# A hybrid decoder layer on one core: step lists per engine for the cross attention, and another order in the mixer's lists

## What is computed

```python
hn = rms_norm(h, norm1_g); proj = hn @ w_in
mix = concat([hgrn2_group(...4 heads...), swa_group(...8 heads, window 128...)]) @ w_out
h = h + mix
hn, mn = rms_norm(h, norm2_g), rms_norm(mem, mem_norm_g)
q = head_rms(hn @ wq, q_norm_g)                        # 4 heads of 128
k, v = head_rms(...mn @ wkv...), ...                   # 256 memory rows
p = softmax(q @ k.T * 128**-0.5)
h = h + (p @ v) @ wo
hn = rms_norm(h, norm3_g); a = relu(hn @ mlp_up)
h = h + (a * a) @ mlp_down
```

## Time and profile before

| | |
|---|---|
| median of 3 runs | 2525.46 us (2523.58 to 2527.55) |
| the profiled execution | 2525.87 us, of which the span of the profile is 2524.1 us |
| granted TensorE clock, mean over the span | 0.996 of 2.4 GHz |
| PE busy | 2465.3 us, 98% of the span |
| PE weight loads busy | 2016.1 us, 80% |
| DVE busy | 1742.6 us, 69% |
| ACT busy | 1138.6 us, 45% |
| POOL busy | 894.0 us, 35% |
| DMA | 371.54 MB, mean 147 GB/s |

### The profile page before, as it was taken

One profiled execution on the slowest core, in us unless ns is written; L12 is line 12 of the kernel. 1 busy time (PEld: TensorE's weight loads), 2 busy tenths in 40 slices (PEclk: granted clock), 3 DMA queues, 4 the chain that ended last, 5 costly groups with the idle time before them and its releaser, 6 DMA issues.

```text
span 2524.1 us, 39349 instructions
## 1 busy us (share of the span) xinstructions
PE 2465.3 (98%) x14110; PEld 2016.1 (80%) x14110; DVE 1742.6 (69%) x3014; ACT 1138.6 (45%) x2164; POOL 894.0 (35%) x1018
## 2 busy tenths in 40 slices
PE   7999999999998999899999999999999999999999
PEld 5877888888887778687878888788888888888887
DVE  6898788788678465666586866976664544566665
ACT  5565576576566356446563222532223233322331
POOL 1433100000001552465246767476673222222222
PEclk9999999999999999999999999999999999999999
DMA  4432633533642431642153344233347653444664
GB/s 185 167 119 103 213 132 120 209 127 120 211 133 105 175 117 59 241 176 76 53 202 109 122 155 158 88 118 127 116 138 268 216 162 107 140 128 148 212 192 142
DMA packets 186547, 371.54 MB, mean 147 GB/s; under 512 B 13937, under 2 KB 79985, under 8 KB 183665
## 3 DMA queue, kind: packets, MB, share of 16 engines
q1 hardware_dynamic: 181200, 359.51, 42.4%
q10 hardware_dynamic: 5152, 9.51, 1.0%
HBM read 286.71 MB, written 79.89 MB: 145 GB/s over the span
## 4 chain that ended last, share of the span: by engine, by line
PE 49%; POOL 5%; issue 5%; DVE 4%; ACT 2%; DMA 2%; SPq 0%; ACTq 0%; DVEq 0%; POOLq 0%
PE bank L3239 8%; PE bank L3241 8%; PE bank L3243 8%; PE bank L3219 4%; PE bank L3215 4%; PE bank L3216 4%; PE bank L2158 3%; PE bank L2153 3%; PE bank L2154 3%; POOL m_xlo L2706 2%; POOL wlo L2706 2%; DMA raw<-w_cross 1%; PE bank L2205 1%; PE bank L2184 1%; PE bank L2195 1%
## 5 line engine op out<-in xcount | busy, mean ns | idle before, releaser
L443 POOL TENSOR_TENSOR wlo<-raw,whi 128x256 fp32r<-128x256 f32 x372 | 326.4, 910 | 960.6 <-ACT whi L1145 520.7
L1538 PE MATMUL bank<-hi,whi 128*128 128x512 f32 x704 | 286.0, 406 | 2.1 <-ACT fg L1108 2.1
L3239 PE MATMUL bank<-hi,whi 128*128 128x512 f32 x896 | 275.8, 389 | 0.0
L3241 PE MATMUL bank<-lo,whi 128*128 128x512 f32 x896 | 275.8, 389 | 0.0
L3243 PE MATMUL bank<-hi,wlo 128*128 128x512 f32 x896 | 275.8, 389 | 0.0
L1541 PE MATMUL bank<-lo,whi 128*128 128x512 f32 x704 | 275.1, 391 | 0.0
L3030 DVE TENSOR_TENSOR lo<-h,hi 128x1024 fp32r<-128x1024 f32 x80 | 124.1, 1552 | 172.7 <-ACT hi L2794 172.6
L2725 POOL TENSOR_TENSOR wlo<-h,whi 128x256 fp32r<-128x256 f32 x160 | 128.8, 829 | 299.3 <-ACT whi L2786 299.3
L2153 PE MATMUL bank<-hi,whi 128*128 128x512 f32 x504 | 208.4, 414 | 13.0 <-DVE h L2046 6.4
L2154 PE MATMUL bank<-lo,whi 128*128 128x512 f32 x504 | 197.8, 393 | 0.0
L3241 PEld LDWEIGHTS bank<-lo,whi 128*128 128x128 f32 x896 | 168.2, 188 | 34.9
(11 more groups left out here) (401 smaller groups left out, 5582.3 us busy)
## 6 DMA issues: line engine op xcount, KB each, us to landing
h<-hidden_scratch SPq DMA_DIRECT2D x96, 512.0 KB, 4.2
raw<-w_mix SPq DMA_DIRECT2D x88, 512.0 KB, 4.2
raw<-w_cross SPq DMA_DIRECT2D x64, 512.0 KB, 3.5
raw<-w_mlp SPq DMA_DIRECT2D x64, 512.0 KB, 4.8
wlo<-mixer_lows_scratch SPq DMA_DIRECT2D x60, 512.0 KB, 3.6
hidden_scratch<-hT SPq DMA_DIRECT2D x116, 256.0 KB, 2.1
h<-w_mlp SPq DMA_DIRECT2D x112, 256.0 KB, 2.9
mixer_lows_scratch<-wlo SPq DMA_DIRECT2D x22, 512.0 KB, 3.0
```

What stands on the lines that cost most here:

```text
L443: last = pool.tensor_tensor(wlo[:, i, cols], raw[:, i, cols], whi[:, i, cols].bitcast(F32), ALU.subtract)
L1538: pe.matmul(out, w, hi[:, k, :], start=k == 0, stop=False)
L3239: pe.matmul(down_bank(i)[:], wh[:, cols], xh[:, i % 2, :], start=K == 0, stop=False)
L3241: pe.matmul(down_bank(i)[:], wh[:, cols], xl[:, i % 2, :], start=False, stop=False)
```

## The change

Mixer: 12 of the 15 lists of PE, ACT and DVE (those of all four blocks; the three start lists and POOL's stay) hold the same steps in another order. Cross: `cross_steps`, `last_squares_end` and `CROSS_WORK` go; `CROSS_ORDERS` has a list for each engine and turn, in which each of PE, ACT and DVE has only its own steps, and `cross_order` yields them. A "-" behind a step in the list of turn 1 means that it belongs to turn 0. No step, no instruction of a step, no wait, buffer or semaphore is added or removed; a wait's threshold stands in the step, so it moves with it. The lists of SP and POOL are the same, instruction by instruction. Lines behind the lists move by 4 (L2046 of before is L2050).

```diff
 ORDERS = {
     "PE": (
...
-        "m0.0 m0.1 s0.0 s0.1 n0 T0 m0.2 m1.0 m1.1 D0 s0.2 s0.3 m1.2 m2.0 m2.1 o0.0 o0.1 o0.2 o0.3 m2.2 L0 m3.0 n1 "
...
+        "m0.0 m0.1 T0 n0 s0.0 s0.1 D0 s0.2 s0.3 m0.2 m1.0 m1.1 m1.2 m2.0 m2.1 m2.2 o0.0 o0.1 o0.2 o0.3 V L0 m3.0 m3.1 "
...
-def cross_steps():
...
-CROSS_STEPS = [s for steps in cross_steps() for s in steps]
-CROSS_WORK = [(turn, s) if s[0] != "late" else (turn - 1, s[1:]) for turn in range(SEQ // TB // 2)
-              for s in CROSS_STEPS if turn or s[0] != "late"]
-CROSS_WORK = last_squares_end(CROSS_WORK)
...
+CROSS_ORDERS = {
+    "PE": (
...
+        "c1.0.0 c1.0.1 u0.2.1 m23.2 u0.3.0 p0.2.0 p0.2.1 n1.2 u0.3.1 c1.1.0 p0.3.0 p0.3.1 n1.3 m24.0 m24.1 m24.2 "
+        "m25.0 m25.1 m25.2 m26.0 m26.1 m26.2 u1.0.0 m27.0 m27.1 m27.2 u1.0.1 c1.1.1 c1.2.0 p1.0.0 p1.0.1 c1.2.1 "
...
+def cross_order(engine):
+
+    for turn, row in enumerate(CROSS_ORDERS[engine]):
+        for token in row.split():
+            step = token.rstrip("-")
+            yield turn - (step != token), (CROSS_NAMES[step[0]],) + tuple(int(n) for n in step[1:].split(".") if n)
...
-            for turn, step in CROSS_WORK:
+            for turn, step in cross_order("ACT"):
...
-            for turn, step in CROSS_WORK:
+            for turn, step in cross_order("DVE"):
...
-            for turn, step in CROSS_WORK:
+            for turn, step in cross_order("PE"):
```

More of the change, by code:

```diff
@@ L230 @@
 CROSS_PRODUCT_AT = {p[1:]: n for n, p in enumerate(CROSS_PRODUCTS)}
-def cross_steps():
-    def panels(role, b, first, end):
-        return list(panel_steps([CROSS_PANEL_AT[role, b, n] for n in range(first, end)],
-                                lambda i: [n for n, p in enumerate(CROSS_PRODUCTS) if p[0] == i]))
-    def squares(b):
-        return [[("norm_square", b, k)] for k in range(KT)]
-    def apply(b):
-        return [[("norm_apply", b, k)] + [("norm_low", b, k - 1)] * (k > 0) for k in range(KT)] + [[("norm_low", b, KT - 1)]]
-    def write(b):
-        return [[("norm_write", b, k)] + [("norm_store", b, k - 1)] * (k > 0) for k in range(KT)] + [[("norm_store", b, KT - 1)]]
-    def attend(b):
-        subs = [(b, u, q) for u in range(HEADS) for q in range(QT // 2)]
-        for n in range(len(subs) + 3):
-            if n < len(subs):
-                yield [("scores", *subs[n])]
-            if 0 <= n - 1 < len(subs):
-                yield [("scale", *subs[n - 1])] + [("turn", *subs[n - 2])] * (n > 1)
-            if n == len(subs) + 1:
-                yield [("turn", *subs[n - 2])]
-            if n >= 3:
-                yield [("pv", *subs[n - 3])] + [("att_out", *subs[n - 3][:2])] * subs[n - 3][2]
-    def squared(steps, role, b, norm):
-        pending = []
-        for group in steps:
-            yield group + pending
-            pending = [("norm_square", norm, CROSS_PRODUCTS[s[1]][3]) for s in group
-                       if s[0] == "take" and CROSS_PRODUCTS[s[1]][1:3] == (role, b)]
-        yield pending
-    def q_norm(b, u):
-        return [[("q_norm", b, u)], [("q_end", b, u)]]
-    late = [[("late",) + s for s in steps] for steps in [[("norm_root", 3)]] + write(3)]
-    yield from spread(panels("out", 0, 0, KT // 2), late)
-    yield from spread(panels("out", 0, KT // 2, KT), [[("split", 1, k)] for k in range(KT)] + squares(0)[:KT // 2])
-    yield from spread(panels("out", 1, 0, 2), squares(0)[KT // 2:] + [[], [], [("norm_root", 0)]])
-    yield from spread(panels("out", 1, 2, KT), spread(apply(0), squares(1)[:KT // 2]))
-    yield from spread(panels("xq", 0, 0, 1), squares(1)[KT // 2:])
-    yield from spread(panels("xq", 0, 1, 2), [[], [("norm_root", 1)], []] + apply(1)[:3] + q_norm(0, 0))
-    yield from spread(panels("xq", 0, 2, 3), apply(1)[3:6] + q_norm(0, 1))
-    yield from spread(panels("xq", 0, 3, 4), apply(1)[6:] + q_norm(0, 2))
-    queries = []
-    for u in range(HEADS):
-        queries += panels("xq", 1, u, u + 1)
-        queries += q_norm(1, u - 1) if u else q_norm(0, 3)
-    yield from spread(list(attend(0)), queries)
-    yield from q_norm(1, HEADS - 1)
-    yield from squared(weave(attend(1), panels("xo", 0, 0, KT // 2), range(21)), "xo", 0, 2)
-    yield from squared(spread(panels("xo", 1, 0, KT // 2), [[("norm_root", 2)]] + write(2) + [[("split", 0, k)] for k in range(KT)]),
-                       "xo", 1, 3)
@@ L297, in last_squares_end @@
-def last_squares_end(work):
-    end = SEQ // TB // 2 - 1
-    late = [(end, ("norm_square", 3, k)) for k in range(KT // 2, KT)]
-    return [s for s in work if s not in late] + [(end, ("mlp_panel",))] + late
-CROSS_STEPS = [s for steps in cross_steps() for s in steps]
-CROSS_WORK = [(turn, s) if s[0] != "late" else (turn - 1, s[1:]) for turn in range(SEQ // TB // 2)
-              for s in CROSS_STEPS if turn or s[0] != "late"]
-CROSS_WORK = last_squares_end(CROSS_WORK)
-CROSS_RMS = [("norm%d" if s[0] == "norm_root" else "q%d%d") % s[1:] for s in CROSS_STEPS
-             if s[0] in ("norm_root", "q_norm")] + ["norm3"]
+CROSS_NAMES = {
[3 rows of a table added]
@@ new lines @@
+CROSS_ORDERS = {
[22 rows of a table added]
+    ),
+    "ACT": (
[17 rows of a table added]
+    ),
+    "DVE": (
[17 rows of a table added]
+    ),
+}
+def cross_order(engine):
[3 more added lines that the diff above has]
+            yield turn - (step != token), (CROSS_NAMES[step[0]],) + tuple(int(n) for n in step[1:].split(".") if n)
+CROSS_RMS = [("norm%d" if s[0] == "norm_root" else "q%d%d") % s[1:] for turn, s in cross_order("PE")
+             if turn == 0 and s[0] in ("norm_root", "q_norm") and s != ("norm_root", 3)] + ["norm3"]
```

## The result

The changed kernel takes **2505.93 us** (median of 4 runs, 2505.24 to 2508.17) against 2525.21 us for the kernel before (4 runs): a ratio of 0.9926, 95% interval 0.9914 to 0.9938. Measured again later, the same pair gave 0.9926 (0.991 to 0.9941). The profiled execution took 2505.29 us with a span of 2503.5 us. The total was forecast as 2506. The stretches were not: the forecast hit the sum by errors of opposite sign.

The account below looks back on a forecast made before the run. PE was taken as the bound nearly everywhere, losing time where needed steps stand behind waiting ones. Terms -6 + 0.5 - 2 - 2.5 - 4.5 - 5 = -19.5 us on 2525.9 gave 2506.4, predicted as 2506 us; range 2491 to 2519.

Parts of the forecast that it names:

- Block 0, -6: Mixer's block 0: shorter waits for ACT's copies of turns and less clock loss gain 6 us (0 to 12).
- a wait of about 1.3 us takes the place of one of 2.8 with its clock: Block 0, head 2's scores: a shorter wait for DVE replaces the largest wait, 2.77 us; 3 us gained (0 to 5.5).
- 3 us forecast around head 3: Block 0, four turns in a row: scores put between them gain 3 us with the clock (0 to 6).
- lists tight where POOL works: Rival: POOL's work delays DVE, block 0 gains only 1 us and cross gains halve; 2517 us, chance 0.15.
- Blocks 1 and 2: Mixer's middle blocks: nothing to gain, +0.5 us (0 to +6) for block 1's chain of state updates.
- Block 3, -2: Mixer's last block: one long wait becomes two shorter ones and some clock returns, 2 us gained (0 to 7).
- Turn 0 up to the third norm, -2.5: Cross stage, turn 0: waits at two totals and in attention shrink, 2.5 us gained (0 to 4).
- in attention 0.6 us and a few of that size: Cross turn 0: the attention waits counted as at stake, beside two totals of 1.4 us.
- Third norm and boundary, -4.5: Cross turn 0 to 1: earlier norm writes let loads start sooner, 4.5 us gained (0 to 10).
- 7 2/3 short products: Third norm's total to turn 1's product 2: PE's short products of 2.72 us, within 32.2 us of own work.
- T + 25.8 + 12.9: Boundary: after `h` and a panel, `hT` follows, so product 2 starts 38.7 us after the third norm's total (T).
- Turn 1, -5: Cross turn 1: the same waits at two totals, third norm's read-outs and attention shrink, 5 us gained (1 to 7).

Follow-up runs that it names:

- tail_old: Changed kernel with the cross stage's steps from the last attention output to product 9 of the next turn in the old order; 2512.98 us, ratio 0.9950.
- block0_mended: Changed kernel with five steps of block 0 moved on PE and DVE, meant to remove four new waits; 2507.45 us, ratio 0.9943.

## Why the prediction came out

**The total was right by cancelling, which is luck.** The mixer was put at -7.5 us and measured at -1.5 in time (-2.1 by stretches); the cross stage at -12 and measured at -17.4 (-19.7 by stretches).

**Block 0, -6, measured -2.6.** The step "a wait of about 1.3 us takes the place of one of 2.8 with its clock" failed in its wait: the scores of head 2 waited 2.63 us, twice the forecast. Its 3 us came all the same, nearly all from the clock. Before, the granted clock is 0.83 from 180 to 190 us and 0.82 from 190 to 200, 3.5 us lost; after, it is 1.00 in both. The 3 us forecast around head 3 came in part: PE is idle as long from 220 to 240 us (3.0 before, 2.9 after, where values p2 now waits), but the clock from 230 to 240 went from 0.83 to 1.00, 1.7 us. What the forecast had at nothing were new waits ahead of head 2, of 1.2 us for the gate's total, 1.65 for scores c4 and some smaller: idle time from 100 to 180 us rose from 1.4 to 5.1 us, 1.5 of it head 2's. Adding up the waits that a new order removes, with what replaces one of them, isn't enough where DVE is late everywhere. The rival "lists tight where POOL works" named the cause: with POOL's work out, old and new lists take 190.5 and 190.2 us. It had put block 0 at -1 and the cross stage at half its gain; the first was nearly so, the second wrong. So its mechanism is shown for block 0, and its time, 2517, was wrong.

**Blocks 1 and 2** went as forecast, without a wait. **Block 3, -2, measured +0.7.** One long wait did become shorter ones, and some of the clock came back (0.98 to 0.99), but there were more of them than two, and idle time rose by 0.8 us. No gain is shown over fourteen profiles.

**Turn 0 up to the third norm, -2.5, measured -6.6** (-4.9 up to the start of product 32). The term that was mis-sized is "in attention 0.6 us and a few of that size". From product 16 to product 32 there were 2.9 us of waits in six entries of 0.3 to 0.6, and another 2.2 us in matmuls that ran longer, which no list of waits holds. For block 0 the prediction had refused to go by the gaps alone; for attention it did just that, for want of a clean stretch to compare with. The changed kernel now gives one: 108.7 us.

**Third norm and boundary, -4.5, measured -7.5** (-9.2 from the start of product 32). The chain was followed right but for two things. The "7 2/3 short products" behind the total hold for the new list; in the old one 7 1/3 stand behind it, so the old list lost 12.0 us here and not 11.1. And one link was wrong. `h` was asked for 16.4 us behind the total (forecast 14; one write waited 0.9 us for a store), and `hT` 6.4 us behind `h`, before that had landed, as forecast. But the step "T + 25.8 + 12.9" lets `hT` start behind the landing of `h`. In fact product 2 began 13.1 us behind the *asking* for `hT`, at 22.8 + 13.1 = 35.9, nearly the 12.9 us of before; the two transfers overlapped:

```profile
h<-xT SPq DMA_DIRECT2D x1, 2048.0 KB, 9.8
hT<-mixed_scratch SPq DMA_DIRECT2D x1, 2048.0 KB, 10.0
```

Neither took longer than a load of `h` before (10.8 us). The forecast kept "10 us if `hT` comes alone and faster" as its far bound; the true value lay between. What was left of the wait moved to product 7, since SP's list puts a load of 2 MB ahead of that panel; the forecast never asked which wait is next once product 2 is early.

**Turn 1, -5, measured -5.6**, with -4.7 in attention, -3.4 from product 32 to product 39 and +2.8 from product 2 to product 8 (by the products' starts); the last the term did not have. Of the forecast's signs, blocks 1 and 2 and the asking for `hT` before `h` had landed came as said. Block 0 at 197.9 (190 to 197 forecast), block 3 at 173.8 (near 171) and the cross turns, shorter by 10.1 and 9.6 us (5 to 7 each), missed. The wait for the read-out right behind the norm's total is gone (one of 0.5 us is left, at product 38); the longest wait is for ACT's `whi`, but at product 7, with 2.6 us, and not at product 2 with 5 to 7.

## What to carry over

Read a stretch's busy time for the same number of matmuls before costing its waits: what a better order is worth shows there, and a list of the long waits holds only a part. Where POOL and DVE both work from SBUF, the length of one POOL operation sets how late a DVE operation can come, so cut POOL's work into short pieces before mending orders; in block 0 mended orders mostly moved the waits. (Short pieces were run for block 0 alone, not for the cross stage, where POOL is busy 105 and 111 us a turn.) And a wait removed counts only with what it does to the granted clock: block 0 got shorter with more idle time at full clock, and longer with less.

## What the chip did that I had not expected

- One DVE operation of 256 columns took 2.57 instead of 0.42 us because a POOL operation of 2.47 us had begun 0.18 us earlier.
- The clock does not follow from the length of one wait. In the profile after, the 2.63 us at head 2 left it at 1.00; in another profile of the same kernel the same wait of 2.63 us brought it to half for a part of the stretch from 180 to 190 us, 0.83 in the mean:

```profile
180.00:190.00 10.00, 8.29 (x116) 7.35 (x116) 9.67 (x22) 5.02 (x12) 3.01 (x4) 1.00 0.44 155
```

```profile
180.00:190.00 10.00, 9.26 (x110) 8.38 (x112) 9.28 (x21) 4.36 (x10) 2.63 (x4) 0.83 0.41 144
```

  In `block0_mended` a wait of 1.98 us went with 0.83 over ten us. In `tail_old` the one of 4.28 us went with 0.83 over the twenty us from 1050 to 1070, 3.4 us lost, where the 3.64 us of before lost 1.7. So a term for the clock of a wait between 2 and 3 us is worth a range, not a value.
- Two loads of 2 MB asked for 6.4 us apart landed in 9.8 and 10.0 us.
